# Two transformer blocks on one core: each residual branch is ended and the next one begun tile by tile, with a product by a diagonal in place of scaling and transposing

## The chip, the core and the metric

The kernel runs on one core of a Trainium2 chip. The metric is the device time of one launch in microseconds, lower is better. Each core has a matmul engine (TensorE, PE in the profile), a vector engine (VectorE, DVE), a scalar engine for activation functions (ScalarE, ACT), GpSimd (POOL) and a queue engine that issues most transfers (SyncE, SP). Matmul results land in eight PSUM banks of 128 partitions by 512 float32; everything else lives in SBUF.

## What is computed

Three residual layers on 256 tokens of width 1024, float32, one after the other. Each has a mixer and a feed-forward part, and every one of these six branches has the same frame:

```python
h = modulate(rms_norm(x, g_pre), shift, scale)   # (h * (1 + scale) + shift)
y = branch(h)
x = x + gate * rms_norm(y, g_post)
```

with `rms_norm(y, g) = y * rsqrt(mean(y*y, -1) + 1e-6) * g`. The branches in their order: neighbourhood attention beside a gated linear recurrence, then `w_out`; a mixture of 16 experts (22.5 MB of gate and up weights and 11.3 MB of down weights each, 32 tokens per expert); a hybrid of delta rule and grouped attention, then `hyb_w_out`; a SwiGLU feed-forward of width 2816; a conformer convolution with a layer norm, SiLU and `conf_w_out` plus `conf_b_out`; a second SwiGLU feed-forward. `shift`, `scale` and `gate` come from a condition vector through `w_mod`.

## The kernel before

The 256 tokens are two tiles of 128 rows (`TT = 2`); `x` stays in SBUF as `X[:, t, :]`. A branch's result `(t, c)` is one PSUM bank: tile `t`, half `c` of the 1024 columns. Weights stream through a ring of six slots of 12 KB per partition; SP refills a slot when PE has read the one six places before. Every engine's program is written out by hand, and engines meet by semaphores (`bank_filled`, `bank_drained` and one per intermediate); an engine runs its program strictly in order. In the three layers the weights of the next stage are fetched while the present one computes, as far as six slots reach.

The frame between two branches is the same everywhere:

1. PE ends the branch: `project_rows` (L518) or `ffn` (L547), with the last accumulation of all four banks close together. In `project_rows` both halves of the mixer's rows (attention heads and readout rows) are transposed first, then columns `c = 0` and `c = 1` are projected.
2. ACT squares the four banks and sums along the rows (`sum_psum`, L2487), DVE adds the halves and makes the mean square (`post_psum`, L1607; `rms_scale`, L1558), ACT takes the root (`root`, L2467), DVE the reciprocal, then `y * r * gate` and `x +`, tile 0 and then tile 1. After the experts and after the conformer, `post` (L1594) does it from SBUF rows; for the conformer DVE first copies each bank out and adds the bias.
3. ACT squares `x` of both tiles, DVE and ACT make one root for both (`normalise`, L1566 and L2481), and DVE scales tile 0 while ACT scales tile 1.
4. PE transposes the scaled rows (`normalised_T`, L479), 16 transposes of 128 x 128, then in two places spreads the gates over the partitions (`modulation_gates`). DVE and ACT apply scale and shift on the way out of PSUM (`modulated_T`), DVE features 0 to 3 and ACT 4 to 7, and PE waits for all of them before the next stage's first matmul (`transposed`).

The last branch ends with one transfer of `X` to memory. A function that ACT evaluates needs its table: `Sqrt`, `Silu`, `Exp` and `Sigmoid` are in different ones here, `Square`, `Copy` and `Identity` in all, and a load stands where the order of ACT's instructions needs another table.

The nine places that matter here are called by the tag of what begins there: `out1` (first out projection, L504), `x2` (the router and the experts, L812), `x3` (after the last expert's `combine`, L866; the hybrid's projections, L1164), `out2` (L504), `f0` (first feed-forward, L561, its down projection L588), `x4` (the conformer's L1425), the conformer's out projection (L1491), `f1` (second feed-forward, L561), and the end.

## Time and profile before

| | us |
|---|---|
| median of 3 runs | 2816.46 |
| lowest and highest run | 2814.12, 2825.08 |
| span of the profiled execution | 2823.3 |
| PE busy in it | 2173.8 (77%) |
| DVE busy | 612.2 (22%) |
| ACT busy | 346.2 (12%) |
| transfers: 755.76 MB, mean 268 GB/s | 67.3% of 16 engines' span |

The profile gives the span of its execution, 2823.3 us, and no separate time of its own; the run nearest to it took 2825.08 us. The span is the stretch from the first to the last instruction, and what lies around it is at most the 1.8 us between these two, if they are the same execution. The page cuts the span in 40 slices: in slices 9 to 25 (some 560 to 1840 us, the experts) the transfers are busy in full at about 420 GB/s; before and after them PE is busy most of the time and the transfers from a tenth to seven tenths.

### The profile page before, as it was taken

What the parts mean: (1) busy time and instruction counts of PE and PEld (TensorE: products, weight loads), DVE (VectorE), ACT (ScalarE), POOL (GpSimd) and SP (SyncE); (2) the same over time, 40 slices, a digit from 0 to 9 for tenths busy, and PEclk for the clock granted to TensorE, in tenths of its full rate; (3) what the DMA queues carried; (4) which work ended last, traced back from release to release, by engine and by line L of the source; (5) the groups of instructions that cost most, each with busy time, mean ns of one, the idle gap of its engine ahead of it and who ended that gap; (6) DMA issues with size and microseconds to landing.
All of it is one profiled execution on the core that took longest, in us unless ns stands there. A gap on an engine that the chain in (4) does not pass through costs nothing.

```text
span 2823.3 us, 36524 instructions
## 1 busy us (share of the span) xinstructions
PE 2173.8 (77%) x16244; PEld 1251.5 (44%) x16244; DVE 612.2 (22%) x1102; ACT 346.2 (12%) x644; POOL 103.7 (4%) x111
## 2 busy tenths in 40 slices
PE   5999786755566666677888855598987998967998
PEld 2344463312222232233445412264775873735873
DVE  1201653200111110121222200354431000721000
ACT  2001321000010000010101000122421000121000
POOL 0001100000000000001111100000300000100000
PEclk9999897999999999999999999897999999888999
DMA  8444712699999999999999999835513453303450
GB/s 337 172 172 172 261 56 80 282 422 424 425 425 421 422 423 416 421 407 424 424 424 424 424 424 425 332 106 183 176 31 108 157 207 102 102 20 96 156 202 22
DMA packets 158892, 755.76 MB, mean 268 GB/s; under 512 B 12233, under 2 KB 75721, under 8 KB 102033
## 3 DMA queue, kind: packets, MB, share of 16 engines
q1 hardware_dynamic: 158736, 753.44, 67.3%
q8 instruction: 128, 2.10, 0.3%
q14 instruction: 28, 0.22, 0.0%
HBM read 752.35 MB, written 1.05 MB: 267 GB/s over the span
## 4 chain that ended last, share of the span: by engine, by line
PE 51%; DMA 38%; DVE 5%; ACT 3%; issue 2%; POOL 0%; DVEq 0%; SPq 0%; ACTq 0%; POOLq 0%
DMA ring<-w_up_dram 15%; PE psum L561 11%; DMA ring<-w_gate_dram 11%; PE psum L504 10%; DMA ring<-w_down_dram 8%; PE psum L588 5%; DMA ring<-hyb_w_dram 3%; PE psum L1056 3%; PE psum L445 2%; PE psum L1425 2%; PE psum L424 2%; PE psum L1120 2%; PE psum L1164 2%; PE psum L1261 1%; PE psum L895 1%
## 5 line engine op out<-in xcount | busy, mean ns | idle before, releaser
L1056 PE MATMUL psum<-ring,arena 128*32 128x320 f32 x4096 | 360.4, 469 | 281.8 <-DMA ring<-w_up_dram 142.5
L561 PE MATMUL psum<-arena,ring 128*128 128x256 f32 x1408 | 308.7, 383 | 5.4 <-issue 5.4
L1056 PEld LDWEIGHTS psum<-ring,arena 128*32 128x32 f32 x4096 | 112.1, 111 | 441.6 <-DMA ring<-w_up_dram 174.7
L1120 PE MATMUL psum<-ring,arena 128*32 128x512 f32 x1344 | 212.9, 609 | 106.1 <-DMA ring<-w_down_dram 106.1
L561 PEld LDWEIGHTS psum<-arena,ring 128*128 128x128 f32 x1408 | 270.4, 192 | 43.6 <-issue 6.0
L504 PE MATMUL psum<-ring,arena 128*128 128x512 f32 x608 | 274.7, 614 | 13.1 <-ACT arena L2504 5.0
L504 PEld LDWEIGHTS psum<-ring,arena 128*128 128x128 f32 x608 | 119.1, 198 | 165.4 <-issue 165.4
L424 PE MATMUL psum<-consts,arena 128*128 128x128 f32 x550 | 100.7, 330 | 112.1 <-DVE arena L1575 71.5
L1120 PEld LDWEIGHTS psum<-ring,arena 128*32 128x32 f32 x1344 | 47.8, 110 | 246.6 <-DMA ring<-w_down_dram 171.1
L424 PEld LDWEIGHTS psum<-consts,arena 128*128 128x128 f32 x550 | 80.5, 179 | 166.6 <-DVE arena L1575 70.6
L588 PE MATMUL psum<-ring,arena 128*128 128x512 f32 x352 | 152.8, 597 | 0.0
L2149 DVE TENSOR_TENSOR arena<-arena,psum 128x320 f32<-128x320 f32 (+1 forms) x32 | 16.7, 521 | 579.5 <-PE psum L1056 573.6
L1065 PE MATMUL psum<-ring,arena 128*32 128x64 f32 x2048 | 120.0, 291 | 0.0
L1065 PEld LDWEIGHTS psum<-ring,arena 128*32 128x32 f32 x2048 | 69.2, 111 | 83.9 <-issue 78.8
L588 PEld LDWEIGHTS psum<-ring,arena 128*128 128x128 f32 x352 | 67.5, 192 | 84.1 <-issue 84.1
L445 PE MATMUL psum<-ring,cols 128*32 128x512 f32 x576 | 89.3, 727 | 19.8 <-DMA ring<-w_mod_dram 17.6
L1713 DVE TENSOR_TENSOR arena<-arena,psum 128x512 f32<-128x512 f32 x22 | 15.1, 688 | 296.6 <-PE psum L561 296.6
L949 PE MATMUL psum<-arena 128*128 128x128 f32 x544 | 73.0, 283 | 1.3
L949 PEld LDWEIGHTS psum<-arena 128*128 128x128 f32 x544 | 64.3, 191 | 16.6 <-issue 16.6
L2773 ACT COPY arena<-psum 128x512 f32<-128x512 f32 x32 | 18.7, 585 | 408.0 <-PE psum L1120 407.9
L2762 ACT ACTIVATE arena<-psum 128x320 f32<-128x320 f32 (+1 forms) x32 | 14.9, 464 | 376.5 <-PE psum L1056 372.4
L866 PE MATMUL psum<-arena 128*128 128x512 f32 x128 | 59.2, 605 | 0.8 <-issue 0.8
(344 smaller groups left out, 1974.6 us busy)
## 6 DMA issues: line engine op xcount, KB each, us to landing
ring<-w_gate_dram SPq DMA_DIRECT2D x128, 1376.0 KB, 18.1
ring<-w_up_dram SPq DMA_DIRECT2D x128, 1376.0 KB, 18.1
ring<-w_down_dram SPq DMA_DIRECT2D x112, 1536.0 KB, 19.9
ring<-w_mod_dram SPq DMA_DIRECT2D x72, 1024.0 KB, 5.0
ring<-w_ffn_in_dram SPq DMA_DIRECT2D x88, 512.0 KB, 5.0
ring<-w_ffn_out_dram SPq DMA_DIRECT2D x14, 1536.0 KB, 6.6
ring<-w_in_dram SPq DMA_DIRECT2D x16, 1024.0 KB, 5.8
ring<-hyb_w_dram SPq DMA_DIRECT2D x10, 1024.0 KB, 16.8
```

The lines of the kernel that those rows point to most:

```text
L424: return nc.tensor.transpose(o, i, const("ident")[0:i.shape[0], 0:i.shape[0]])
L445: ins = nc.tensor.matmul(psum[32 * j:32 * j + 32, bank, :], stat, w[:, j, :], start=(k == 0), stop=(k == KT - 1), skip_group_check=True)
L504: ins = nc.tensor.matmul(banks[t][:, 0:n], XTt(kk, t), w[:, k, :], start=(kk == 0), stop=(kk == 7), skip_group_check=True)
L561: ins = nc.tensor.matmul(b[:, i * 256:(i + 1) * 256], ws[k // 4][:, k % 4, u, i * P:(i + 1) * P], R(XT + k * 256, 256), start=(k == 0), st ...
L588: ins = nc.tensor.matmul(banks[2 * t + c], R(HTF + k * 256 + t * P, P), w[:, (k % 3) * D + c * HALF:(k % 3) * D + (c + 1) * HALF], start=( ...
L866: ins = nc.tensor.matmul(b, R(SALL + e * 256 + t * P, P), R(YS + c * HALF, HALF), start=True, stop=True, skip_group_check=True)
L949: ins = nc.tensor.matmul(result(tag)[:, h * P:(h + 1) * P], lhs(h), rhs(h), start=True, stop=True, skip_group_check=True)
L1056: ins = nc.tensor.matmul(banks[u][c][32 * j:32 * j + 32, 0:GMAIN], R(XST + k * HALF + e * CAP, CAP), w3[:, 64 * c:64 * c + 64, QGROUP * j: ...
L1065: ins = nc.tensor.matmul(banks[u][1][32 * j:32 * j + 32, GMAIN:GMAIN + GEXTRA], R(XST + k * HALF + e * CAP, CAP), extra, start=False, stop ...
L1120: ins = nc.tensor.matmul(ybanks[half][32 * c:32 * c + 32, :], stationary, w, start=((half, c) not in begun), stop=(unit >= 36), skip_group ...
L1164: ins = nc.tensor.matmul(b[:, 0:SEQ], w[:, k, f * P:(f + 1) * P], R(XT + k * 256, SEQ), start=(k == 0), stop=(k == 7), skip_group_check=True)
L1425: ins = nc.tensor.matmul(b[:, i * 256:(i + 1) * 256], ws[k // 4][:, k % 4, u, i * P:(i + 1) * P], R(XT + k * 256, 256), start=(k == 0), st ...
```

## The change

All six branch ends and the five beginnings behind them are redone, and both out projections:

- **Ends, tile by tile** (`end_tile`). DVE multiplies a bank by the gate as soon as it is full, ACT squares it, the root is taken per tile with the mean square's first half as its bias, and one DVE instruction per half does `x + r * (y * gate)`, `x_half_ready` after the first half.
- **Beginnings.** ACT squares the halves of `x`, the root and reciprocal are per tile, DVE writes `diag(r)` (`unit_diagonal`), and PE multiplies the unscaled rows of `x` by it (`scaled_T`), which scales and transposes at once. PE waits per feature (`feature_arrived`), no longer for all. The gates are spread by PE before tile 0's products and after them.
- **Order in the banks.** The down projection's last four k steps run bank by bank, so that the four banks fill one after the other. The out projections run in halves: the heads half (transposed earlier, `heads_T`) for all four banks first, then the readout rows' half bank by bank. In the conformer the bias is a product with a row of ones, and the first four features are used as they come.
- **Table loads** are asked for earlier (`preload_act_table`).
- **The end**: three transfers, tile 0 and the two halves of tile 1.

The core of the diff:

```diff
+            def scaled_T(tag, gates_of=None):
+                if gates_of:
+                    modulation_gates(gates_of, (0,), 6)
+                for t in range(TT):
+                    pe.wait_ge(diagonal_ready, tally.due(diagonal_ready))
+                    for h in range(2):
+                        bank = next_bank((tag, t, h))
+                        if nth((tag, t, h)) > 1:
+                            pe.wait_ge(bank_drained[bank_of((tag, t, h))], nth((tag, t, h)) - 1)
+                        for i in range(4):
+                            k = 4 * h + i
+                            ins = nc.tensor.matmul(bank[:, i * P:(i + 1) * P], X[:, t, k * P:(k + 1) * P], diagonal(t),
+                                                   start=True, stop=True, skip_group_check=True)
...
+                    if t == 0 and gates_of:
+                        modulation_gates(gates_of, (1,))
...
-            def project_rows(tag, mixes):
...
+            def project_rows(tag, heads_half, heads_at, mixes):
...
+                for c in range(2):
+                    enlist((tag, c, heads_half))
...
+                    for t in range(TT):
+                        for k in range(4):
+                            ins = nc.tensor.matmul(banks[t, c], R(heads_at + k * 256 + t * P, P), w[:, k, :],
+                                                   start=(k == 0), stop=False, skip_group_check=True)
...
+                rows_T(0)
...
+                for t in range(TT):
+                    pe.wait_ge(bank_drained[bank_of((tag, "T", t))], nth((tag, "T", t)))
+                    for c in range(2):
...
+                        for k in range(4):
+                            ins = nc.tensor.matmul(banks[t, c], R(XT + k * 256 + t * P, P), w[:, k, :], start=False,
+                                                   stop=(k == 3), skip_group_check=True)
...
+                        if t == c == 0:
+                            rows_T(1)
...
+                for t in range(TT):
+                    for c in range(2):
+                        for k in range(3 * n_slots - 6, FT):
...
+            def end_tile(t, tags, zt, g):
+
+                first, second = tags(t, 0), tags(t, 1)
+                if t:
+                    v.wait_ge(x_ready, tally.given[x_ready])
+                v.wait_ge(bank_filled[bank_of(first)], nth(first))
+                weigh(result(first), 0, zt, g).then_inc(branch_weighed, 1)
+                tally.gave(branch_weighed)
+                mean_square_base(644 + t, 640 + 2 * t)
+                v.wait_ge(square_sum_ready, tally.due(square_sum_ready))
+                weigh(result(second), 1, zt, g).then_inc(bank_drained[bank_of(second)], 1)
...
+                inverse_root(712 + t)
+                add_branch(t, zt)
+
+            def unit_diagonal(t):
+                v.wait_ge(square_sum_ready, tally.due(square_sum_ready))
+                v.wait_ge(root_ready, tally.due(root_ready))
+                inverse_root(654 + t)
+                v.tensor_scalar(diagonal(t), const("ident"), sm(654 + t, 1), None, ALU.mult).then_inc(diagonal_ready, 1)
...
+            def end_and_begin(tags, zt, g, tag, scale_at, shift_m):
+                end_tile(0, tags, zt, g)
+                mean_square_base(650, 646)
+                unit_diagonal(0)
+                end_tile(1, tags, zt, g)
+                begin_second(tag, scale_at, shift_m)
+
+            def begin_second(tag, scale_at, shift_m):
+                features(tag, 0, scale_at, shift_m)
+                mean_square_base(651, 648)
+                unit_diagonal(1)
+                features(tag, 1, scale_at, shift_m)
...
+            def end_and_begin(tags, jk, tag, scale_at, shift_m):
+                end_tile(0, tags, jk)
+                begin_tile(0, jk)
+                end_tile(1, tags, jk)
+                features(tag, 0, scale_at, shift_m)
+                begin_tile(1, jk)
+                features(tag, 1, scale_at, shift_m)
...
-            s.wait_ge(out_ready, tally.due(out_ready, 2))
-            s.dma_start(out.rearrange("(t p) n -> p t n", p=P), X).then_inc(stored, 16)
+            s.wait_ge(x_ready, tally.due(x_ready, 7))
+            s.dma_start(rows_out[:, 0, :], X[:, 0, :]).then_inc(stored, 16)
+            s.wait_ge(x_half_ready, tally.due(x_half_ready, 12))
+            s.dma_start(rows_out[:, 1, 0:HALF], x_half(1, 0)).then_inc(stored, 16)
+            s.wait_ge(x_ready, tally.due(x_ready))
+            s.dma_start(rows_out[:, 1, HALF:D], x_half(1, 1)).then_inc(stored, 16)
```

The first `end_and_begin` is DVE's, the second ACT's. How the rows stand on an engine is shown at three places; a name in brackets is the semaphore that the instruction waits for, and `x7` means seven more like it.

PE at `out1` and `x2`, before: L424 are transposes, L504 the projection, L812 the router.

```order
L424 MATMUL psum<-consts,arena 128x128 [waits bank5_drained]
L424 MATMUL psum<-consts,arena 128x128 x3
L504 MATMUL psum<-ring,arena 128x512 [waits bank0_drained,bank5_drained,bank1_drained,bank4_drained,slot4_loaded,bank3_drained,bank2_drained]
L504 MATMUL psum<-ring,arena 128x512 x7
L504 MATMUL psum<-ring,arena 128x512 [waits slot5_loaded]
L504 MATMUL psum<-ring,arena 128x512 x7
L504 MATMUL psum<-ring,arena 128x512 [waits slot0_loaded,bank3_drained,bank2_drained]
L504 MATMUL psum<-ring,arena 128x512 x7
L424 MATMUL psum<-consts,arena 128x128 [waits bank4_drained,normed_ready]
```

The same place with the change: L579 is the heads half, L436 the transposes of the readout rows, L599 their half, L510 the products by the diagonal.

```order
L579 MATMUL psum<-ring,arena 128x512 [waits slot5_loaded]
L579 MATMUL psum<-ring,arena 128x512 x7
L436 MATMUL psum<-consts,arena 128x128 [waits bank2_drained,mix_ready]
L436 MATMUL psum<-consts,arena 128x128 x3
L599 MATMUL psum<-ring,arena 128x512 [waits slot0_loaded,bank2_drained]
L599 MATMUL psum<-ring,arena 128x512 x3
L436 MATMUL psum<-consts,arena 128x128 [waits bank3_drained,mix_ready]
L436 MATMUL psum<-consts,arena 128x128 x3
L599 MATMUL psum<-ring,arena 128x512 [waits slot1_loaded]
L599 MATMUL psum<-ring,arena 128x512 x3
L510 MATMUL psum<-diagonals,x 128x128 [waits bank4_drained,diagonal_ready]
```

Sixteen of the 32 matmuls now stand ahead of the wait for `mix_ready`, and one bank is ended before the second tile's rows are transposed.

PE at the conformer's end, before: L1474 are the layer norm's sums, L1491 the out projection.

```order
L1474 MATMUL psum<-arena,consts 128x256 [waits bank6_drained,conf_var_in]
L1474 MATMUL psum<-arena,consts 128x256 x7
L1491 MATMUL psum<-ring,arena 128x512 [waits bank0_drained,slot0_loaded,bank7_drained,conv_out_ready]
L1491 MATMUL psum<-ring,arena 128x512 x7
L1491 MATMUL psum<-ring,arena 128x512 [waits slot1_loaded]
L1491 MATMUL psum<-ring,arena 128x512 x7
```

With the change: L1591 are the bias products, L1603 the first features' half, each of its first four with a wait of its own for `conv_out_ready`, L1615 the other half.

```order
L1591 MATMUL psum<-arena,consts 128x512 [waits bank0_drained,out_bias_loaded]
L1591 MATMUL psum<-arena,consts 128x512 [waits bank1_drained]
L1603 MATMUL psum<-ring,arena 128x512 [waits conv_out_ready,slot0_loaded]
L1603 MATMUL psum<-ring,arena 128x512 [waits conv_out_ready] x3
L1603 MATMUL psum<-ring,arena 128x512 x4
L1603 MATMUL psum<-ring,arena 128x512 [waits slot1_loaded]
L1603 MATMUL psum<-ring,arena 128x512 x7
L1615 MATMUL psum<-ring,arena 128x512 [waits slot2_loaded,conv_out_ready]
L1615 MATMUL psum<-ring,arena 128x512 x3
L1615 MATMUL psum<-ring,arena 128x512 [waits slot3_loaded]
L1615 MATMUL psum<-ring,arena 128x512 x11
L510 MATMUL psum<-diagonals,x 128x128 [waits bank4_drained,diagonal_ready]
```

The wait for all eight features has become a wait for one at a time.

ACT between the conformer and the second feed-forward, before: L2476 squares rows, L2469 is the root, L2484 scales tile 1, L2504 are the features.

```order
L2476 ACTIVATE arena,small<-arena 128x1024 [waits bank2_drained,bank0_drained,square_sum_ready]
L2469 ACT_TABLE_LOAD [waits mean_square_ready]
L2469 ACTIVATE small<-small 128x2 [waits square_sum_ready]
L2476 ACTIVATE arena,small<-x 128x1024 [waits x_ready,root_ready]
L2476 ACTIVATE arena,small<-x 128x1024 [waits square_sum_ready]
L2469 ACTIVATE small<-small 128x2 [waits mean_square_ready,square_sum_ready]
L2484 ACTIVATE arena<-x,small 128x1024 [waits rms_ready,root_ready]
L2504 ACTIVATE arena<-psum,modcol,shsc 128x128 [waits bank0_filled,normed_second_ready]
```

With the change, from the second tile's end on: L2645 squares a half, L2652 is the root of one tile, L2676 are the features.

```order
L2645 ACTIVATE arena,small<-psum 128x512 [waits branch_weighed,root_ready]
L2645 ACTIVATE arena,small<-psum 128x512 [waits bank3_filled]
L2652 ACTIVATE small<-small 128x1 [waits mean_square_ready,square_sum_ready]
L2676 ACTIVATE arena<-psum,modcol,shsc 128x128 [waits bank5_filled,bank2_drained]
L2676 ACTIVATE arena<-psum,modcol,shsc 128x128 x3
L2645 ACTIVATE arena,small<-x 128x512 [waits x_half_ready]
L2645 ACTIVATE arena,small<-x 128x512 [waits x_ready]
L2652 ACTIVATE small<-small 128x1 [waits mean_square_ready,square_sum_ready]
L2676 ACTIVATE arena<-psum,modcol,shsc 128x128 [waits bank1_filled,root_ready]
L2676 ACTIVATE arena<-psum,modcol,shsc 128x128 x3
L3166 ACT_TABLE_LOAD
```

The table load has left the place between the sums and the root, tile 0's features stand ahead of tile 1's squares of `x`, and the features wait for one another no longer.

## Rows read from the trace of the kernel before

**Rows 1.** The page's part 4: shares of the chain that ended last, by engine.

```profile
PE 51%; DMA 38%; DVE 5%; ACT 3%; issue 2%; POOL 0%; DVEq 0%; SPq 0%; ACTq 0%; POOLq 0%
```

**Rows 2.** The chain in order of time, first block: start us, us, engine, line, instructions.

```profile
417.16 2.81 PE psum L795 x32
431.85 29.15 PE psum L504 x64
478.80 6.72 PE psum L812 x32
```

**Rows 3.** Timeline of PE at the second feed-forward's start: start us, us, what, idle before.

```profile
2555.52 4.45 PE L1491 MATMUL psum<-ring,arena 128*128 128x512 f32 x10
2573.47 3.67 PE L424 MATMUL psum<-consts,arena 128*128 128x128 f32 x16 [13.50 <-DVE arena L1575]
2579.74 2.47 PE L561 MATMUL psum<-arena,ring 128*128 128x256 f32 x5 [2.60 <-issue]
```

**Rows 4.** Timeline of ACT at the same place: the root of the branch's sums.

```profile
2562.42 1.28 ACT L2469 ACT_TABLE_LOAD   x1 [0.38 <-DVE small L1559]
2563.71 0.20 ACT L2469 ACTIVATE small<-small 128x2 f32<-128x2 f32 x1
```

**Rows 5.** Single lines: count, ns min/median/max, first and last start, shapes.

```profile
L2491 ACT ACTIVATE arena<-psum x16: 597/597/597, 443.9 to 2810.2; 128x512 f32<-128x512 f32 x16
L1553 DVE TENSOR_TENSOR gates<-psum,arena x12: 691/692/692, 214.2 to 2410.6; 128x512 f32<-128x512 f32 x12
L1618 DVE SCALAR_TENSOR_TENSOR arena<-psum,small,gates x16: 750/751/752, 462.8 to 2816.9; 128x512 f32<-128x512 f32 x16
L1584 DVE TENSOR_SCALAR arena<-psum,shsc,modcol x64: 409/410/411, 43.3 to 2577.8; 128x128 f32<-128x128 f32 x64
L2504 ACT ACTIVATE arena<-psum,modcol,shsc x64: 457/457/459, 43.4 to 2579.0; 128x128 f32<-128x128 f32 x64
L748 PE MATMUL psum<-arena x32: 275/275/347, 388.2 to 391.8; 128*128 128x128 f32 x32
```

**Rows 6.** Windows of 2 us: busy by engine, granted TensorE clock (PEclk), DMA share, GB/s.

```profile
2563.00:2565.00 2.00, 0.00 (x0) 0.00 (x0) 0.95 (x2) 0.90 (x2) 0.00 (x0) 0.91 0.86 305
2585.00:2587.00 2.00, 2.00 (x10) 1.77 (x9) 0.00 (x0) 0.00 (x0) 0.00 (x0) 0.97 0.00 0
```

**Rows 7.** Window from the first block's out projection to its first expert.

```profile
464.00:516.00 52.00, 28.75 (x109) 17.89 (x113) 24.38 (x53) 8.82 (x16) 0.00 (x0) 0.67 0.04 15
```

**Rows 8.** Chain: the second block's out projection and first feed-forward (columns as in Rows 2).

```profile
2107.79 29.15 PE psum L504 x64
2154.83 153.89 PE psum L561 x704
```

**Rows 9.** Chain: both down projections and the conformer's start.

```profile
2312.76 76.96 PE psum L588 x176
2410.69 57.35 PE psum L1425 x256
2734.58 75.55 PE psum L588 x176
```

**Rows 10.** Timeline of PE and chain: the last combine of experts and the hybrid's start.

```profile
1805.29 3.67 PE L866 MATMUL psum<-arena 128*128 128x512 f32 x8 [0.79 <-issue]
1828.84 13.24 PE psum L1164 x48
```

**Rows 11.** Timeline of ACT and PE before the conformer's out projection.

```profile
2524.24 1.28 ACT L2950 ACT_TABLE_LOAD   x1 [4.26 <-DVE arena L2453]
2525.53 5.03 ACT L2950 ACTIVATE arena<-arena,cols 128x256 f32<-128x256 f32 x8
2530.61 2.92 PE L1491 MATMUL psum<-ring,arena 128*128 128x512 f32 x3 [12.96 <-ACT arena L2950]
```

**Rows 12.** Timeline of SP at the end, and the page's landing time of that transfer.

```profile
2818.90 0.39 SPq L3225 DMA_DIRECT2D out_dram<-x  x1
out_dram<-x SPq DMA_DIRECT2D x1, 1024.0 KB, 4.0
```

475 lines of the change are left out of this document (300 added, 175 removed).

## Prediction

> **What bounds the kernel.** I read the shares of the chain that ended last first: PE has 51% of it and the transfers 38%, the vector and scalar engines 8% together [rows 1]. So a change of orders on DVE and ACT pays only where PE stands still with nothing else to do, and that is at the branch ends. The timeline there shows it: PE's last projection matmul ends at 2559.97 (2555.52 + 4.45), it is idle 13.50 us, transposes for 3.67, is idle again, and begins the next stage at 2579.74 [rows 3]. From the last matmul to the next stage's first that is 19.8 us, nearly all DVE and ACT in turn. Every entry of the sum below is such a distance: what it is in the chain or timeline before, what the new order makes of it. I write T for the end of a branch's last matmul.
>
> **Prices.** A 512-column square out of PSUM 0.60, gate times bank 0.69, an add or scale of 512 columns 0.75, a DVE feature 0.41, an ACT feature 0.46, a product of 128 columns 0.24 (32 instructions from 388.2 to 391.8 are 16 source matmuls, since a float32 product issues two) [rows 5]. The same PE work at 1.2 GHz takes about double. A 512-column source matmul takes 75.55 / 88 = 0.86 (176 instructions) [rows 9]. A root or another instruction on a few columns takes 0.20, a table load 1.28 [rows 4]. A hand-off between engines takes 0.05 to 0.1 (ACT ends at 2530.56, PE begins at 2530.61) [rows 11]. The diagonal, 128 columns with its reciprocal, is in no row; its bounds are two small instructions (0.4) and a DVE feature plus a small one (0.6), hand-offs beside them. Between a 128-column operation from SBUF and one from PSUM I take 0.3 + 0.2.
>
> **The common frame.** Before, everything starts after T. With the banks filling one after the other, 4 source matmuls or 3.43 us apart, tile 0's banks are full at T-10.3 and T-6.9; its weighing, squares, root, adds, squares of `x` and diagonal (some 8.5 us of work) lie under the other two banks' matmuls. If that cover went, tile 0's end would stand in front, and most of the gain would be lost. Behind T remains tile 1's second half: weigh and square to T+1.6, root and reciprocal to T+1.9, two adds to T+3.4. PE meanwhile multiplies tile 0 (T to T+1.9), ACT does its features and is free at T+4.0; the squares of the two halves of `x` end at T+5.4, root T+5.7, diagonal T+6.3, PE's first half-bank T+7.3, first feature T+7.85, first matmul T+7.9.
>
> **The sum.**
> - *f1*: 19.8 [rows 3] becomes 7.9: 11.9.
> - *f0*: 2107.79 + 29.15 = 2136.94, next stage at 2154.83 [rows 8], so 17.9 becomes 7.9: 10.0.
> - *x4*: 2312.76 + 76.96 = 2389.72, conformer at 2410.69 [rows 9]: 21.0. The gates' products and DVE's three evictions at 0.7 are in that; now half of them stand before tile 0's products, the other half between the tiles. I take 8.9: 12.1.
> - *out1*: from 419.97 (417.16 + 2.81) to 461.00 (431.85 + 29.15), 41.0 [rows 2]. Now 16 source matmuls (13.7) start at once, under them the readout is finished by DVE (it ended before 431.85), then four transposes and a copy, 1.2, and the late half with four more transposes, 14.2: 29.2. Gain 11.8. The 8 transposes of the heads and two copies are added earlier, at 8 x 0.24 + 2 x 0.7 = 3.3 if all is in the way, 0 if none is. At out1 they stand among the modulation's products, whose weights PE waits for, and I take 0.
> - *out2*: the same projection, 29.15 [rows 8], gain 11.8; there the transposes stand directly ahead of the delta rule's chain, and I take PE's part, 1.9: 9.9.
> - *x2*: T = 461.00, router ends at 485.52 (478.80 + 6.72) [rows 2], 24.5. Now the products end at T+8.3, or at T+10.1 at half clock; the router's 16 source matmuls take 3.4 or 6.7 behind them: T+11.7 to T+16.8. I take 13.8, nearer full clock, since tile 0's products come right behind T: 10.7. The load of the table for `Exp` is asked for earlier, 1.3. Together 12.0.
> - *x3*: T = 1808.96 to 1828.84 [rows 10], 19.9. All four banks fill in 3.7 us, so there is no cover, and DVE is the chain: 4 combines, 4 weighings, 4 adds (8.8), some ten small ones (2.0), 4 features (1.6), a diagonal (0.3), then ACT's second square, PE's products and the first feature (2.5), a dozen hand-offs (1.0) and half a table load (0.6), 16.8, of which hardly anything lies before T. I take 16.7: 3.2, with 2 to 6 as bounds.
> - *Conformer*: SiLU starts at 2525.53 behind a table load at 2524.24, PE at 2530.61 behind all eight features [rows 11]. Without this load and one ahead of it on ACT (2 x 1.28) and with a wait per feature, PE starts at about 2523.7; 32 source matmuls, 27.4, end at 2551.1 and not 2559.97: 8.9. The two bias products lie in PE's 12.96 us of idle time; without that they cost 1.7.
> - *End*: T = 2734.58 + 75.55 = 2810.13 [rows 9], transfer issued at 2818.90, landing 4.0 later [rows 12]. Now the last issue is at T+3.4 (5.4 won), and 256 KB in place of 1024: I estimate 2.1 for it from the 4.0 (bounds 1.0, a quarter, and 4.0): 1.9. Together 7.3.
> - *Clock*: TensorE's granted clock fell to 1.2 GHz within the idle stretch (0.91 of full over 2563 to 2565) and was back only in 2585 to 2587, over 5 us after PE had begun L561 [rows 6]. Some 1.5 to 2.7 us are lost so at a boundary. The new gap is T+1.9 to T+6.4, 4.5 us; here some 4.7 had passed between PE's last matmul and the fall, so the rows leave open on which side it comes out. I count half of what three boundaries lose: 3.0. Bounds: 0 and 6.
>
> Sum: 11.9 + 10.0 + 12.1 + 11.8 + 9.9 + 12.0 + 3.2 + 8.9 + 7.3 + 3.0 = 90.1. Gains before the experts, where the transfers bound, could be taken back; but from 464 to 516 the queues are busy only 4% [rows 7], so the weights don't run ahead there and both terms pass in full. Against the span of 2823.3 that is 2733; the profiled execution lies 0.2% above the median, and against the median of 2816.46 it is 2726, my forecast. Its own range is 2712 to 2740 (clock -3 or +3, x3 and x2 each 3, each boundary 1 either way, out1 and out2 3).
>
> **Two rules against rows.** Without the load ACT's root follows it at once: 2562.42 + 1.28 = 2563.70, root at 2563.71 [rows 4]. The Trainium skill (ScalarE: Activation LUTs, section What ACT_TABLE_LOAD costs) states 1283 ns and a drain of 1380 ns for every switch, 2.66 us; the load agrees, the drain doesn't show here, and the measurement decides. By the page's sum the two loads of the conformer would be worth 2.8 more.
>
> The products at L748 took 0.24 each at full clock, 16 transposes at half clock 3.67, so 0.23 each [rows 3, 5]: scaled to one clock a product is about twice a transpose. If it were four times (0.46), 16 products would take 7.4 in place of 3.8, and if all are in the way each of five boundaries would be 3.6 later, 18 together: 2744. The Trainium skill (TensorE: Matmul & The Clock Gate, section Terms) says that transpose mode is "4× faster for FP32", which speaks against the diagonal; the trace bears it out by half.
>
> **Rivals.**
> - *The chain is dearer than its rows*: DVE and ACT hand over some fifteen times per tile, tile 0's end isn't done at T, and tile 1's weighing is late. The first matmul stands at T+11 at five boundaries: 15 less won, 2741. For: DVE's order puts tile 0's diagonal ahead of tile 1's weighing. Against: 10.3 us of cover for 8.5 us of work. 0.14.
> - *The experts take back the start* (weights not there when the router is early): 11.8 + 12.0 less, 2750. Against: the 4% [rows 7]. 0.05.
> - *Products at four transposes*: 2744, against the row of L748. 0.03.
> - *Better*: the clock stays up at all boundaries (+3), the features come earlier, out1's readout was later than I think: about 2712 and under. 0.06.
> - *Slower*: the first matmuls of a stage are now paced by features that come one at a time, and PE stays at 1.2 GHz for long. Each us at half clock costs 0.5. It decides when the four stages behind f0, x4, f1 and x3 each spend over 52 us at half clock, since then 4 x 0.5 x (52 - 5) = 94 eats the sum; with 60 each it gives 110 and 2836. Against: with all features ready the clock was up in over 5 us [rows 6], and pacing lasts under 4. 0.02.
> - *It doesn't do what it says*: tile 0's end waits for something that comes after T (a bank not drained, a wait for all), and the end is serial as before; out1 and out2 alone give little if the readout is late: about 2816, no change. 0.02.
>
> **Chances.** The forecast has 0.68. 0.5% is 14 us, about what a measurement of this kernel can tell from no change. Faster by more: 0.96, same 0.02, slower 0.02. The range takes in the dearer chain, the products at four transposes and the experts' case with a little of the sum's own spread on top, and the better side down to 2708: 2708 to 2752.
>
> **What the profile after would show.** Right: PE's gap behind each T, 11.6 to 13.5 us before, is about 4.5 us between tile 0's and tile 1's products; the next stage's first matmul at T+8; at out1 and out2 the heads half directly behind the last delta-rule matmuls (L795's) and not 12 us later; no table load between sums and root; the last transfer issued at T+3.4; a granted clock near 1 earlier behind each start. Wrong: gaps of over 8 us, matmuls of the last banks that stand apart, an expert stage longer than before, a table load that has only moved onto the path, PE at half clock for more than 10 us behind a start.

## The result and the profile after

| | before | with the change |
|---|---|---|
| median of the runs, us | 2817.03 (4 runs) | 2730.06 (4 runs, 2725.39 to 2732.89) |
| ratio to before | | 0.9686, 95% interval 0.9669 to 0.9702 |
| profiled execution, us | (not given) | 2729.94 |
| its span, us | 2823.3 | 2728.1 |

The forecast was 2726.0, its range 2708 to 2752. The median fell by 87.0 us and the span by 95.2; the forecast's sum was 90.1. The chain of the changed kernel, by engine, for [rows 1]:

```profile
PE 53%; DMA 39%; DVE 4%; ACT 2%; issue 1%; POOL 0%; DVEq 0%; SPq 0%; ACTq 0%; POOLq 0%
```

DVE and ACT have gone from 8% to 6% of a shorter span. The chain in order of time (start us, us, engine, line, instructions), for [rows 2, 8, 9, 10, 11]; L579 and L599 are the halves of the out projections, L669 and L686 the down projection and its last four k steps, L1603 and L1615 the conformer's out projection:

```profile
419.69 13.93 PE psum L579 x32
...
438.92 10.30 PE psum L599 x24
...
458.48 3.57 PE psum L915 x32
473.88 16.42 PE psum L944 x32
...
1801.67 11.17 PE psum L1269 x48
...
2063.71 13.93 PE psum L579 x32
...
2082.95 10.30 PE psum L599 x24
...
2101.42 153.08 PE psum L641 x704
...
2321.51 13.73 PE psum L686 x32
...
2345.49 55.52 PE psum L1531 x256
...
2470.92 13.73 PE psum L1615 x32
...
2494.00 153.04 PE psum L641 x704
...
2708.84 13.75 PE psum L686 x32
```

A reader takes the ledger from these lines: the end of a branch's last matmul, then the first of the next stage. L599 ends at 449.22, and behind it the router ends at 462.05; L686 ends at 2335.24 and the conformer begins at 2345.49. T' is T for the conformer: the end of L1615, 2484.65. Set against the rows of before:

| stretch | before | after | won | forecast |
|---|---|---|---|---|
| start to the delta rule's last matmul | 419.97 | 419.69 | 0.3 | 0 |
| out1: from there to T | 41.0 | 29.5 | 11.5 | 11.8 |
| x2: T to the gather behind the router | 37.4 | 24.7 | 12.7 | 12.0 |
| experts | 1310.6 | 1310.6 | 0.0 | 0 |
| x3: T to the hybrid | 19.9 | 17.2 | 2.7 | 3.2 |
| hybrid and out2 | 308.1 | 291.6 | 16.5 | 9.9 |
| f0: T to L641 | 17.9 | 8.2 | 9.7 | 10.0 |
| first feed-forward | 234.9 | 233.8 | 1.1 | |
| x4: T to L1531 | 21.0 | 10.3 | 10.7 | 12.1 |
| conformer to T' | 149.3 | 139.2 | 10.1 | 8.9 |
| f1: T' to L641 | 19.8 | 9.4 | 10.4 | 11.9 |
| second feed-forward | 230.4 | 228.6 | 1.8 | |
| end | 13.2 | 5.5 | 7.7 | 7.3 |
| clock, not assigned to a stretch | | | | 3.0 |

The column "won" adds up to the 95.2 of the spans, not to the 87.0 of the medians. The profiled execution of before has a span of 2823.3 against a median of 2817.03 (it is the slowest of the four if it is the run of 2825.08), and the one with the change lies at its median. So some 8 us of the column belong to which execution was profiled, and the rows don't say in which stretch they lie.

The timeline of PE at the second feed-forward's start (start us, us, what, idle before), for [rows 3]:

```profile
2484.49 1.95 PE L510 MATMUL psum<-diagonals,x 128*128 128x128 f32 x16
2490.22 3.78 PE L510 MATMUL psum<-diagonals,x 128*128 128x128 f32 x16 [3.79 <-DVE diagonals L1752]
2493.80 3.46 PE L641 MATMUL psum<-arena,ring 128*128 128x256 f32 x10
```

The 13.50 us of idle time have become 3.79, between the products of tile 0 and of tile 1 (16 instructions are 8 products). What DVE and ACT do in those 3.79 us, DVE first:

```profile
2485.41 0.69 DVE L1715 TENSOR_TENSOR arena<-psum,gates 128x512 f32<-128x512 f32 x1 [1.28 <-ACT arena L2645]
...
2489.88 0.29 DVE L1752 TENSOR_SCALAR diagonals<-consts,small 128x128 f32<-128x128 f32 x1
2492.34 1.36 DVE L1759 TENSOR_SCALAR arena<-psum,shsc,modcol 128x128 f32<-128x128 f32 x4 [2.17 <-PE psum L510]
```

```profile
2486.53 1.50 ACT L2676 ACTIVATE arena<-psum,modcol,shsc 128x128 f32<-128x128 f32 x4 [0.83 <-PE psum L510]
2487.92 0.64 ACT L2645 ACTIVATE arena<-x 128x512 f32<-128x512 f32 x1
...
2489.29 0.29 ACT L2652 ACTIVATE small<-small 128x1 f32<-128x1 f32 x1
```

DVE ends its second weighing at 2486.10, adds, and makes tile 1's diagonal at 2489.88. ACT's four features of tile 0 (L2676) stand ahead of its squares of tile 1's `x` (L2645), whose second is followed by the root at 2489.29. No table load lies there, where [rows 4] had one. Now the windows of 2 us (busy by engine, then the granted clock, PEclk, and the transfers' share), for [rows 6]:

```profile
2488.00:2490.00 2.00, 0.00 (x0) 0.00 (x0) 1.37 (x7) 1.55 (x6) 0.00 (x0) 0.82 0.70 249
2490.00:2492.00 2.00, 1.78 (x8) 1.78 (x9) 0.17 (x1) 0.00 (x0) 0.00 (x0) 0.50 0.00 0
...
2494.00:2496.00 2.00, 2.00 (x7) 1.55 (x6) 0.00 (x0) 1.88 (x5) 0.00 (x0) 0.50 0.00 0
2496.00:2498.00 2.00, 2.00 (x11) 1.77 (x10) 0.00 (x0) 0.91 (x1) 0.00 (x0) 0.98 0.00 0
```

Even in so short a gap the clock fell to 1.2 GHz. Tile 1's eight products took 3.78 us and tile 0's 1.95; the stage's first matmul began at half clock, and full clock was back in the window from 2496. For [rows 11]: SiLU's table is now loaded at 2450.44 while ACT waits for the layer norm, and SiLU begins at 2454.63, PE at 2455.38. At the end SP issues three transfers, for [rows 12]; the last matmul ends at 2722.59:

```profile
2718.84 0.36 SPq L3445 DMA_DIRECT2D out_dram<-x  x1
2725.03 0.34 SPq L3447 DMA_DIRECT2D out_dram<-x  x1
2725.70 0.33 SPq L3449 DMA_DIRECT2D out_dram<-x  x1
```

### The profile page after: what moved, and what is told of

It reads as the page before. It is cut to its first block, busy times and chain, and to the rows that moved or that the text cites. A ratio compares the mean times of both kernels' runs of the same rounds, so it can differ in the third digit from the quotient of the medians.

```text
span 2728.1 us, 36736 instructions
## 1 busy us (share of the span) xinstructions
PE 2164.0 (79%) x16332; PEld 1249.6 (46%) x16332; DVE 608.0 (22%) x1138; ACT 344.9 (13%) x679; POOL 103.4 (4%) x111
## 4 chain that ended last, share of the span: by engine, by line
PE 53%; DMA 39%; DVE 4%; ACT 2%; issue 1%; POOL 0%; DVEq 0%; SPq 0%; ACTq 0%; POOLq 0%
DMA ring<-w_up_dram 16%; PE psum L641 11%; DMA ring<-w_gate_dram 11%; DMA ring<-w_down_dram 8%; PE psum L543 8%; PE psum L669 5%; DMA ring<-hyb_w_dram 3%; PE psum L1161 3%; PE psum L457 2%; PE psum L1531 2%; PE psum L1225 2%; PE psum L1269 2%; PE psum L436 1%; PE psum L1367 1%; PE psum L1000 1%
## 5 line engine op out<-in xcount | busy, mean ns | idle before, releaser
L641 PE MATMUL psum<-arena,ring 128*128 128x256 f32 x1408 | 306.5, 381 | 0.0
L641 PEld LDWEIGHTS psum<-arena,ring 128*128 128x128 f32 x1408 | 269.8, 192 | 36.4
L543 PE MATMUL psum<-ring,arena 128*128 128x512 f32 x480 | 214.8, 610 | 11.1 <-ACT arena L2698 5.0
L543 PEld LDWEIGHTS psum<-ring,arena 128*128 128x128 f32 x480 | 93.3, 196 | 130.2 <-issue 130.2
L669 PE MATMUL psum<-ring,arena 128*128 128x512 f32 x288 | 125.0, 596 | 0.0
L436 PE MATMUL psum<-consts,arena 128*128 128x128 f32 x470 | 79.8, 307 | 35.5 <-DVE arena L1695 8.6
L436 PEld LDWEIGHTS psum<-consts,arena 128*128 128x128 f32 x470 | 62.2, 166 | 86.4 <-issue 51.8
L669 PEld LDWEIGHTS psum<-ring,arena 128*128 128x128 f32 x288 | 55.3, 192 | 68.5 <-issue 68.4
L2969 ACT COPY arena<-psum 128x512 f32<-128x512 f32 x32 | 18.7, 585 | 405.9 <-PE psum L1225 405.9
## 6 DMA issues: line engine op xcount, KB each, us to landing
ring<-w_gate_dram SPq DMA_DIRECT2D x128, 1376.0 KB, 18.2
ring<-w_down_dram SPq DMA_DIRECT2D x112, 1536.0 KB, 19.9
```

Of the source, the lines that this page charges most:

```text
L436: return nc.tensor.transpose(o, i, const("ident")[0:i.shape[0], 0:i.shape[0]])
L543: ins = nc.tensor.matmul(banks[t][:, 0:n], XTt(kk, t), w[:, k, :], start=(kk == 0), stop=(kk == 7), skip_group_check=True)
L641: ins = nc.tensor.matmul(b[:, i * 256:(i + 1) * 256], ws[k // 4][:, k % 4, u, i * P:(i + 1) * P], R(XT + k * 256, 256), start=(k == 0), st ...
L669: ins = nc.tensor.matmul(banks[2 * t + c], R(HTF + k * 256 + t * P, P), w[:, (k % 3) * D + c * HALF:(k % 3) * D + (c + 1) * HALF], start=( ...
```

## Experiments

The times in brackets behind a place are distances by PE's timeline, whose groups overlap by up to 0.2 us. In the changed kernel they are: T to the router's end 12.82, T to x3's first matmul 16.99, f0 7.96, x4 10.04, f1 9.14, end 5.52. The two theories of the study: what bounds a boundary is the chain of instructions as summed in the prediction; or something that the sum treats as given (the clock, the size of a product, a rule of the Trainium skill) decides.

The kernels of this section were measured in three groups, each on a chip of its own and beside the kernel before. Its median was 2816.46 us in the first group (banks together, scaled rows, tables, heads half), 2821.86 in the second (all features, one transfer, the gap filled with products, squares first) and 2814.16 in the third (the repeat, the two combinations, the gap filled with transposes). A difference of medians across groups is therefore uncertain by some us, and the distances inside a profile carry the readings.

### The changed kernel once more

> The changed kernel once more, as the mark for the three others on the same chip: 2726 to 2733, ratio to the kernel before 0.967 to 0.970. Its distances from one place to the next should repeat within 0.1 us where PE's clock is the same, and differ by up to 1.5 us where it isn't; the hybrid's stage, 256 to 268 us in the nine kernels profiled so far without an edit there, should differ by several us again.

2732.27 us median, ratio 0.9704 (0.9687 to 0.9721); the ratio of one kernel thus came out 0.2% apart, and the two intervals overlap. The distances repeat within 0.05 us at every boundary (12.80, 17.00, 7.99, 10.05, 9.14, 5.55), the clock's falls included. The hybrid's stage took 261.8 us, as in the first profile (262.2); that it would differ by several us was expected and didn't happen.

### Banks of the down projection together

```diff
-                for t in range(TT):
-                    for c in range(2):
-                        for k in range(3 * n_slots - 6, FT):
+                for k in range(3 * n_slots - 6, FT):
+                    for t in range(TT):
+                        for c in range(2):
```

> Undoes one part of the change: the last k steps of both down projections go back to all four banks together, so the banks are full 0.86 us apart and not 3.4. Theory of the forecast (tile 0's end is hidden only because the banks fill apart): at x4 tile 0's end and diagonal stand in front, the first matmul moves from T+10.3 to about T+14 (+3.9), at the end the last transfer from T+3.6 to about T+6.4 (+2.9): 6.8 in all, 2737. Rival (the gain is in fewer waits and the diagonal, the bank order is worth nothing): under 1 us, 2730 to 2731.

2736.63 us median. At x4 the distance is 14.42 in place of 10.04, at the end 8.86 in place of 5.52: 7.7, where 6.8 was expected. PE at x4, by its timeline:

```profile
2327.48 6.17 PE L686 MATMUL psum<-ring,arena 128*128 128x512 f32 x14
...
2337.34 3.65 PE L510 MATMUL psum<-diagonals,x 128*128 128x128 f32 x16 [2.63 <-DVE diagonals L1752]
...
```

Tile 0's products, which had followed the last matmul behind the gates, now wait for a diagonal and start 3.7 us after T (2333.65). The cover is real: this is the price of its absence.

### Scaled rows and transposes

```diff
-    v.tensor_scalar(diagonal(t), const("ident"), sm(654 + t, 1), None, ALU.mult)
+    v.tensor_scalar(R(ROWS_OF[tag] + t * D, D), X[:, t, :], sm(654 + t, 1), None, ALU.mult)
...
-    nc.tensor.matmul(bank[:, i * P:(i + 1) * P], X[:, t, k * P:(k + 1) * P], diagonal(t),
-                     start=True, stop=True, skip_group_check=True)
+    transpose(bank[:, i * P:(i + 1) * P], R(ROWS_OF[tag] + t * D + k * P, P))
```

> Undoes one part of the change: at all five boundaries DVE scales the tile's rows of x (1024 columns) and PE transposes them, in place of the product with the diagonal; the order of all else stays. Costs 0.75 in place of 0.29 on DVE for tile 1, and wins on PE where four products come before the first feature: at 1.2 GHz they take 0.47 each (16 instructions in 3.78) and a transpose 0.23. Theory that a transpose is half a product: 0.46 lost and 0.96 won at each boundary, 2.5 won in all, 2727.5. Forecast's first view, that the diagonal saves as much as it costs or more: 2730 to 2732. By the rule of the Trainium skill (TensorE: Matmul & The Clock Gate, section Terms) of four times for float32: 1.4 won and 0.46 lost each, 2725.

2726.91 us median (2725.24 to 2728.38), 3 below the change, of which the chip's own 0.2% leaves little certain. The distances say more: x3 14.31, f0 7.70, x4 8.10, f1 7.68, so 6.3 won there, but the router's end 14.55, 1.7 lost; and 4.1 were lost behind the boundaries (conformer 112.6 to its out projection in place of 110.1, the three parts of the feed-forwards 157.9, 77.1, 153.8 in place of 157.3, 76.7, 153.1). Why, PE shows at the router:

```profile
448.37 1.04 PE L437 MATMUL psum<-consts,arena 128*128 128x128 f32 x8
454.47 1.97 PE L437 MATMUL psum<-consts,arena 128*128 128x128 f32 x8 [5.06 <-DVE arena L1752]
456.23 6.85 PE L915 MATMUL psum<-cols,arena 128*128 128x16 f32 x32
```

Eight transposes take 1.04 us at full clock and 1.97 at half, 0.13 and 0.25 each, where a product takes 0.24 and 0.47. PE is done with tile 0 sooner (by 0.9) and DVE's scaling of 1024 columns takes longer than the diagonal, so the gap is 5.06 and not 3.79, and the router's matmuls ran at half clock to their end (6.85 in place of 3.75). The ratio of product to transpose is 1.9. The Trainium skill (TensorE: Matmul & The Clock Gate, section Terms) gives transpose mode as four times faster for float32; the rows here don't agree. The theory of half a product had the number, 2727.5, and left out what the longer gap costs.

### Tables loaded where they are needed

```diff
-            a.preload_act_table(ACT.Silu)
...
-            a.preload_act_table(ACT.Sqrt)
```

(all thirteen such lines)

> Undoes one part of the change: no table is asked for early, each load stands directly ahead of the first function that needs it. Five places where the load has no cover (Exp for the router, the roots of both readouts, the layer norm's root, SiLU of the conformer) cost 1.28 each, 6.4; at the other branch ends the root of tile 0 is covered in part and costs about 0.5 each: some 9 us in all, 2739. With the drain that the Trainium skill (ScalarE: Activation LUTs, section What ACT_TABLE_LOAD costs) adds to each, 2.66 in place of 1.28: about 23 us, 2753. Rival (loads lie beside other work whether early or not): 2730 to 2732.

2733.93 us median, 3.9 above the change, where 2739 was expected. In the profile router to gather is 13.10 in place of 11.84 (+1.3, `Exp`), x3 18.01 (+1.0), and the conformer to its out projection 112.8 in place of 110.1 (+2.7). ACT in the conformer:

```profile
2450.06 1.28 ACT L3145 ACT_TABLE_LOAD   x1 [5.94 <-DVE arena L2608]
2451.35 0.42 ACT L3145 ACTIVATE arena<-arena 128x256 f32<-128x256 f32 x1
2456.03 1.28 ACT L3150 ACT_TABLE_LOAD   x1 [4.26 <-DVE arena L2614]
2457.32 3.13 ACT L3150 ACTIVATE arena<-arena,cols 128x256 f32<-128x256 f32 x5
```

Two loads of 1.28, and each is followed by its function within 0.02 us; together they cost the 2.7. That is 1.3 a switch, and no drain shows. By the Trainium skill (ScalarE: Activation LUTs, section What ACT_TABLE_LOAD costs) I estimate 5.3 for the two; the rows here don't agree. ACT had been idle before both, but it is no different right behind work: in the changed kernel's hybrid stage ACT ends a copy at 1963.05, the load (1.28) starts at 1963.07 and the next function at 1964.36. At f0 and x4 the distances are 1.2 longer and 1.3 shorter, which is the clock in tile 1's products (3.78 in place of 2.60, 2.05 in place of 3.42). The other places cost nothing: the load ahead of a readout's root lies beside the heads half (out1 and out2 29.6 as before), and at the branch ends tile 0's end has that much cover (f1 9.15). So of the five places thought to have no cover the two readouts have it, and the 0.5 expected at each of the other branch ends was wrong.

### Heads half not before the readout

```diff
+                pe.wait_ge(mix_ready, tally.had.get(mix_ready, 0) + 1)
                 for c in range(2):
                     enlist((tag, c, heads_half))
```

> Undoes one part of the change: both out projections wait for the readout's first rows before the heads half begins, the order in the banks stays. Theory (the gain is that 13.9 us of matmuls run while the readout is finished): at out1 the heads half starts at about 428.9 and not 419.7, the projection ends about 9 us later, the same at out2: 18 us, 2748. Rival (what counts is that the late half ends bank by bank): under 3 us each, 2736 or less.

2748.23 us median, 18.2 above the change. PE at out1:

```profile
419.12 2.88 PE L896 MATMUL psum<-arena 128*32 128x128 f32 x32
427.76 16.48 PE L580 MATMUL psum<-ring,arena 128*128 128x512 f32 x32 [5.75 <-DVE arena L1993]
```

The heads half starts 5.75 us after the delta rule and at half clock (16.48 in place of 14.00). From the delta rule's end to T it is 37.8 in place of 29.5, 8.3 more, of which 2.5 are clock. The rival, by which the banks' order is what counts, is out.

### All features before the first matmul

```diff
-                if k % 4 == 3:
...
+                if k == 0:
+                    for h in range(2):
+                        pe.wait_ge(bank_drained[bank_of((tag, 1, h))], nth((tag, 1, h)))
```

> Undoes one part of the change: a stage's first matmul waits for all eight features again, in the router, the hybrid's projections, both feed-forwards and the conformer (its out projection's waits for SiLU stay). Theory (PE works on the first features while the last are made): at f1 ACT ends its last feature 1.6 us after PE's first matmul began, so each of four places loses 1.6 to 1.7, the router 0 because the first tile's matmuls lie there: 6.5 us, 2736.5. Rival (PE runs ahead and then waits for the last features, nothing is won): 2730 to 2731.

2742.18 us median, 12 above the change and nearly twice what was expected. f1 is 11.10 (+2.0, where 1.6 to 1.7 was expected), and PE idles 1.75 us between the products and the stage:

```profile
2504.22 3.78 PE L510 MATMUL psum<-diagonals,x 128*128 128x128 f32 x16 [3.79 <-DVE diagonals L1749]
2509.75 4.43 PE L638 MATMUL psum<-arena,ring 128*128 128x256 f32 x11 [1.75 <-ACT arena L2673]
```

x3 is 18.95 (+2.0), x4 11.74 (+1.7) and the router's end 13.20 (+0.4). At f0 it is 11.11 (+3.2), since tile 1's products ran wholly at half clock, and the stages behind lost 0.9 (first feed-forward), 2.1 (conformer) and 0.8 (second): 13 us by place. The extra idle time costs again as clock: the conformer's first stage takes 58.48 us in place of 55.52.

### One transfer at the end

```diff
-            s.wait_ge(x_ready, tally.due(x_ready, 7))
-            s.dma_start(rows_out[:, 0, :], X[:, 0, :]).then_inc(stored, 16)
...
+            s.wait_ge(x_ready, tally.due(x_ready, 8))
+            s.dma_start(rows_out, X).then_inc(stored, 16)
...
```

> Undoes one part of the change: X goes out in one transfer of 1024 KB at the end in place of three. Theory of the forecast: it lands 4.0 us after its issue as before and not about 2 after: from the last matmul to the end 7.4 to 7.7 in place of 5.5, 2732. Rival (a transfer's fixed part is all there is, 256 KB takes as long): 0, 2730.

2732.76 us median (2725.85 to 2740.26), too wide to tell 2 us. The end is 7.54 in place of 5.52: 2.0, as expected, from the profile alone. The page's landing times are 4.0 us for the 1024 KB and 2.0 for 256 KB.

### PE's gap filled with products

```diff
+        FILL = dict(x2=4, x3=0, f0=4, x4=3, f1=4)
...
+                    for _ in range(t * FILL[tag]):
+                        nc.tensor.matmul(first, const("ident"), consts[:, 0:HALF], start=True, stop=True,
+                                         skip_group_check=True)
                     pe.wait_ge(diagonal_ready, tally.due(diagonal_ready))
```

> Adds work that computes nothing: between the products of tile 0 and those of tile 1 PE multiplies a constant, four products of 512 columns (3.4 us at full clock) at x2, f0 and f1, three at x4, none at x3, into the bank that tile 1's products then overwrite. Theory (the gap of 2.7 to 3.8 us is what lets the clock fall; at f1 PE then works 5.9 us at half clock and loses 2.9, at x2, f0 and x4 3 to 3.5 us and loses 1.5 to 1.8): without the gap the clock stays, 7 to 8 us won, 2722. Rival (the clock falls for another reason, or the added matmuls delay the diagonal's product by what they save): 2730 or more.

2714.67 us median, 7 under what was expected, ratio 0.9620 (0.9606 to 0.9635), the interval clear of the change's. By the medians that is 15.4 us won, by the ratios 18.6. PE at f1, then its clock:

```profile
2472.35 1.95 PE L517 MATMUL psum<-diagonals,x 128*128 128x128 f32 x16
2474.14 3.60 PE L508 MATMUL psum<-consts 128*128 128x512 f32 x8
2478.09 2.05 PE L517 MATMUL psum<-diagonals,x 128*128 128x128 f32 x16 [0.35 <-DVE diagonals L1759]
2479.97 6.21 PE L648 MATMUL psum<-arena,ring 128*128 128x256 f32 x28
```

```profile
2478.00:2480.00 2.00, 1.91 (x17) 1.92 (x18) 0.75 (x4) 0.00 (x0) 0.00 (x0) 1.00 0.00 0
```

The clock stays at full, tile 1's products take 2.05, and L648 (the stage) begins at T+7.45, not 9.14. The router ends at 11.10, f0 is 7.47, x4 8.71; the first feed-forward's parts gain 1.5 and 1.0 and the second 1.1, the conformer with its out projection loses 0.6: 8.1 us by place, as expected. The measured gain is larger, and where the rest lies is told below.

### Squares first

```diff
-                features(tag, 0, scale_at, shift_m)
-                begin_tile(1, jk)
+                begin_tile(1, jk)
+                features(tag, 0, scale_at, shift_m)
...
```

> A change of order on ACT and DVE at all five boundaries: ACT squares the halves of tile 1's x ahead of its four features of tile 0 (now behind them, 1.5 us), and DVE makes the mean square's base after two of its features. Theory (ACT is the chain there): tile 1's diagonal is ready 0.6 to 0.7 earlier at each, 3 in all, and the shorter gap can also keep the clock up in part: 2725 to 2727. Rival (tile 0's late features, now ready 1.5 us later, are what PE needs first): 2730 or more.

2725.23 us median (2716.31 to 2729.38), as expected, though four runs that far apart can't bear a difference of 3 us alone. The gaps at x2, f0 and f1 are 3.10 in place of 3.79, the 0.7 of the theory; but the boundaries differ: router's end 14.56 (+1.7), x3 14.80 (-2.2), f0 8.01, x4 6.76 (-3.3), f1 8.33 (-0.8). At x4 the gap shrinks to 0.78 us, the gates' products lying in it, and the clock stays:

```profile
2343.67 2.05 PE L510 MATMUL psum<-diagonals,x 128*128 128x128 f32 x16 [0.78 <-DVE diagonals L1752]
2345.55 4.70 PE L1531 MATMUL psum<-arena,ring 128*128 128x256 f32 x21
```

At x2 the clock fell when PE had just begun again, and the router ran at half. Where no other work fills the gap, an earlier diagonal is not enough.

### Both, and both with transposes

> Two edits together, both from runs before: PE's gap is filled with products of a constant (three at x2, f0 and f1, two at x4, none at x3) and ACT squares tile 1's x ahead of tile 0's features. Theory (with the clock held, the 0.6 us that the squares give at each boundary no longer hide behind a lower clock; alone they cost 1.7 at the router where PE fell to half clock): 3 us below the filled kernel, 2710 to 2713, and the router's end at T+10.5. Rival (the filled gap already has all that the order gives): 2714 to 2716.

> The kernel before this one, and at all boundaries scaled rows and transposes in place of the product with the diagonal. At full clock a transpose takes 0.13 and a product 0.24, so four of them save 0.46, and scaling 1024 columns costs 0.46 more on DVE than the diagonal: nothing won or lost if the clock stays. Theory (transposes count less than products for the clock: with them alone the router's matmuls took 6.66 and not 3.57): the clock falls again at some boundaries, 1 to 2 us each, 2714 to 2720. Rival (PE's work is PE's work, the filling is enough): as the kernel before this one, within 2 us.

2716.63 (ratio 0.9648, 0.9632 to 0.9665) and 2713.61 us (0.9639, 0.9620 to 0.9657), beside 2732.27 for the change on the same chip: 15.6 and 18.7 less. Neither came out as its theory had it: the first was to be 3 us under the filled kernel (2710 to 2713), and the second to lose by the transposes. The router's end is at 10.41, as expected, f0 at 6.78, x4 at 7.63, f1 at 6.77, x3 at 14.93. With transposes 10.61, 6.59, 6.60, 6.60 and 12.73, and the clock at f1 did not fall. So the boundaries win 3.4 again by transposes, and the expected loss of 1 to 2 at each isn't there; 3 were given back in the conformer (112.1 in place of 109.1). Which of these two and the filled kernel is fastest is not settled, their intervals overlap; all three are faster than the change.

### The gap filled with transposes

```diff
-                    for _ in range(t * FILL[tag]):
-                        nc.tensor.matmul(first, const("ident"), consts[:, 0:HALF], start=True, stop=True,
-                                         skip_group_check=True)
+                    for i in range(7 * t * FILL[tag]):
+                        transpose(first[:, i % 4 * P:(i % 4 + 1) * P], const("ident"))
```

(against the kernel filled with products)

> The filled gap again, but with transposes of the identity in place of the products, seven for each (28 at x2, f0 and f1, 21 at x4), about as long (0.13 each, 3.6 us). Theory (transposes don't hold the clock up): PE is busy in the gap and the clock falls all the same, 2727 to 2733 as without any filling. The Trainium skill (TensorE: Matmul & The Clock Gate, Part 4: PE-mode transpose) says that transposes don't count as busy for the clock in the same way, by which it is this outcome. Rival (any work holds it): 2713 to 2717 as with products.

2718.82 us median, 13.5 below the change on the same chip: the theory falls. PE at f1, and a window of its clock:

```profile
2484.46 3.22 PE L437 MATMUL psum<-consts 128*128 128x128 f32 x28
2488.41 2.05 PE L516 MATMUL psum<-diagonals,x 128*128 128x128 f32 x16 [0.73 <-DVE diagonals L1758]
2490.30 4.05 PE L647 MATMUL psum<-arena,ring 128*128 128x256 f32 x18
```

```profile
2488.00:2490.00 2.00, 1.59 (x14) 1.59 (x15) 0.71 (x4) 0.00 (x0) 0.00 (x0) 1.00 0.00 0
```

PEclk is 1.00 when tile 1's products begin: 28 transposes in 3.2 us hold it as the products did: router 11.11, f0 7.47, x4 8.71, f1 7.46, each within 0.02 of the kernel filled with products. The Trainium skill (TensorE: Matmul & The Clock Gate, Part 4: PE-mode transpose) says that transposes don't count as busy for the clock in the same way; the rows here don't agree. So it was not their kind that made the router slow in the kernel with scaled rows, and the longer gap remains as the reason.

## Why the prediction was right

**The frame held** (2733 against a span of 2823.3; measured 2728.1). PE's idle time after T was what there was to win, tile 0's end does lie under the other banks' matmuls (7.7 us without that), the heads half does run under the readout (18.2 us without that), and the experts, 1310.6 us before and after, took nothing back, as the 4% of [rows 7] said.

**Terms that were right for the reason given**: out1 11.5 for 11.8, x2 12.7 for 12.0 (tile 1's products at half clock, the router at full), the end 7.7 for 7.3 (the last transfer was issued 3.1 us after T, and the three together give 2.0 of it).

**That the total came out near is in part luck.** Two terms were 1.4 and 1.5 too large, f0 and x3 near by errors that cancelled, and the stretch with out2 won 6.6 more than its term. The sum's 90.1 lies between the 95.2 of the spans and the 87.0 of the medians.

**f1 and x4 were sized too large** (11.9 and 12.1, measured 10.4 and 10.7). The step that failed is "PE's first half-bank T+7.3, first feature T+7.85, first matmul T+7.9". The diagonal came earlier than summed (products from T+5.57 and not 6.4), and DVE's first feature was there at T+8.1. But PE runs in order: all eight products of tile 1 stand ahead of the stage, and at 1.2 GHz they take 3.78. The first matmul stands at 5.57 + 3.78 = 9.35. At full clock it is 5.57 + 2.05 less the overlap of the records, 7.45 in the filled kernel. At x4 it is 6.83 + 3.42 = 10.25, for 8.9. At f0 the clock fell only within the products (2.60), so it is 5.57 + 2.60 = 8.17 for 7.9, near by two errors that cancelled.

**x3 (2.7 for 3.2) came out near in the same way.** It was summed as DVE's work. PE there:

```profile
1790.32 3.78 PE L510 MATMUL psum<-diagonals,x 128*128 128x128 f32 x16 [4.80 <-DVE diagonals L1752]
...
1797.89 3.78 PE L510 MATMUL psum<-diagonals,x 128*128 128x128 f32 x16 [1.78 <-DVE diagonals L1752]
```

2.5 us of DVE's work lay before T (it begins at 1782.00, T is 1784.47), where the sum had hardly anything. From tile 0's products on the way led over PE at half clock and over ACT, whose squares of tile 1's `x` stand behind its four features; DVE waited 1.95 us for them. Tile 1's products began at T+13.4 and took 3.78. Squares first took 2.2 out of x3 with the same work on DVE.

**The clock's term was too rough.** "I count half of what three boundaries lose: 3.0." The granted clock fell in the gap or just behind it at all five boundaries, where the gaps were 2.7 to 4.8 us long. Filling it brought 8.1 us by place. Yet the stages behind did begin earlier at full clock than before: 1.1 and 1.8 in the feed-forwards, 1.8 of the conformer's 10.1 (L1531 55.52 in place of 57.35), and in the hybrid 2.1 (L1269 11.17 in place of 13.24). The mechanism was right, the place of the gains and losses was not foreseen.

**out2 gained 11.6**, counted as at out1 from the delta rule's last matmul (2095.78 and 2063.71) to T (2136.94 and 2093.25), 41.2 and 29.5 us; the sum had 11.8 for it and took off 1.9 for the transposes of the heads. These stand earlier, in the hybrid's stage and in its chain:

```profile
1968.13 1.91 PE psum L436 x8
```

From the matmuls ahead of them (L941 before, L1046 now) to the delta rule's first (L1261, L1367) it was 4.40 us (1998.61 to 2003.01) and is 5.53 (1967.10 to 1972.63), so they cost 1.1: DVE also copies their banks (1.29) before it goes on. The other 4.9 of the stretch's 16.5 are in the hybrid: 3.4 by the clock in its projections, and 1.5, with that loss taken off, in a stage whose time differs between profiles, as told below.

**Conformer 10.1 for 8.9**: 8.3 without the 1.8 of the clock. The two loads are worth 2.7 by their removal (2.56 counted).

**The rivals**: the dearer chain, the experts, the products at four transposes and the slower side can be put aside by the rows named; half clock ended some 2 us into the stage behind f1 (the window from 2496), and not after 52.

## What to carry to other kernels

Where PE waits for a chain on other engines, end and begin the work tile by tile, so that only the last tile's chain stands behind the last matmul; fill the accumulators one after the other, since that makes the cover. When such a gap has shrunk to a few us, look at the granted clock before shortening the chain further: here a few matmuls on a constant, into a bank that is overwritten next, brought the median down by 15.4 us, and transposes in their place by 13.5 on one chip, more than any rearrangement of the chain that was tried; 8.1 us of it can be shown by place. And sum each engine's queue to the instruction in question, not only to the first operand that arrives.

## What the runs showed that was not expected

The hybrid's stage from its first projection to the heads half took between 256.7 and 268.4 us in the twelve profiles where it does not hold the heads' wait, and hardly an edit lies inside it. Windows over the whole stage (us, then busy by engine and PEclk) of the change, the kernel filled with products, and squares first:

```profile
1801.46:2063.64 262.18, 240.28 (x2329) 170.34 (x2328) 128.17 (x243) 79.85 (x170) 23.83 (x22) 0.91 0.40 134
```

```profile
1798.53:2055.21 256.68, 234.76 (x2330) 167.14 (x2329) 128.16 (x243) 79.91 (x170) 23.83 (x22) 0.94 0.40 136
```

```profile
1800.90:2069.29 268.39, 245.19 (x2330) 175.51 (x2328) 128.39 (x244) 79.91 (x170) 23.83 (x22) 0.90 0.39 132
```

PE's busy time follows the mean granted clock: 0.91, 0.94 and 0.90 with 240.3, 234.8 and 245.2 us; the work is the same. These are different kernels, and the one profiled twice took 262.2 and 261.8, so that it differs from execution to execution is argued and not shown. What speaks for it: single runs of a kernel lie up to 14 us apart (2725.85 and 2740.26 with one transfer), and the profiled execution of the kernel filled with transposes was its slowest, 6.5 us above its median, with this stage 6.3 longer than in the kernel filled with products. If so, one profile's span can hide or add several us of a change whose places agree within 0.1. It also is the likeliest home of what the filled kernels won beyond the 8 us by place, since 5.5 of the filled kernel's span lie there; but the one filled with transposes took 263.0 in it, so with one profile for each kernel this stays open.

DVE's second weighing at a branch's end waits for ACT's square, 0.7 us at five of the six ends (at f1 2485.41 after ACT's square of 2484.69); behind the experts, where the rows lie in SBUF, they run side by side (1782.79 and 1782.85). At the five both read the same PSUM bank, and the kernel keeps them apart; another order wasn't tried.
